# Bidirectional RWKV-7 triangular inverse: the transposed state kept by a vector transpose in place of its own matmuls

## What is computed

```python
def step(S, inp):                       # one token; two directions z, 16 heads of 64 channels
    r_t, w_t, k_t, v_t, a_t, b_t = inp
    sa = jnp.einsum('zbhvk,zbhk->zbhv', S, a_t)
    S = S * w_t[..., None, :] + sa[..., :, None] * b_t[..., None, :] + v_t[..., :, None] * k_t[..., None, :]
    return S, jnp.einsum('zbhvk,zbhk->zbhv', S, r_t)

xs = (shared(r), time_major(decay), time_major(k_dir), shared(v), shared(-kk), time_major(b_dir))
_, ys = lax.scan(step, jnp.zeros((2, B, H, N, N), f32), xs)
```

## Time and profile before

| | us |
|---|---|
| median of 3 runs | 1345.2 |
| lowest and highest | 1340.76, 1352.06 |
| the profiled execution | 1351.68 |
| its span, from first to last instruction | 1349.8 |
| scan stage in it, tile 0 to the end of tile 7 | about 854 to 1105 |

### The profile page before, as it was taken

How to read it: one execution, slowest core, us unless ns; L and a number is a source line. 1 busy time by engine, 2 the same in 40 slices (tenths; PEclk the granted TensorE clock), 3 DMA queues, 4 the chain that set the end, 5 groups by cost and what they waited for, 6 DMA issues and landing times.

```text
span 1349.8 us, 33102 instructions
## 1 busy us (share of the span) xinstructions
PE 1259.2 (93%) x14080; PEld 1131.4 (84%) x14080; DVE 919.8 (68%) x1270; ACT 644.7 (48%) x1045; POOL 442.0 (33%) x220
## 2 busy tenths in 40 slices
PE   8999999999899999899997899888888889899998
PEld 5899999878799999799996898877777777799998
DVE  7666667786877776766667985656555546866654
ACT  5544446452644455644445368233333333555553
POOL 1344442211244443344443000543334303344442
PEclk9999999999999999999998899789999989999999
DMA  8355555323355555455555342010000012555553
GB/s 332 141 185 184 186 185 173 123 86 140 141 186 186 186 186 200 174 186 186 186 186 187 101 181 95 3 50 4 4 4 4 3 50 95 195 188 186 186 184 119
DMA packets 18676, 188.34 MB, mean 140 GB/s; under 512 B 2064, under 2 KB 2576, under 8 KB 3600
## 3 DMA queue, kind: packets, MB, share of 16 engines
q1 hardware_dynamic: 18576, 186.84, 38.5%
HBM read 185.78 MB, written 1.05 MB: 138 GB/s over the span
## 4 chain that ended last, share of the span: by engine, by line
PE 75%; DVE 15%; ACT 5%; issue 3%; POOL 1%; DMA 0%; SPq 0%; DVEq 0%; ACTq 0%
PE gu_bank L257 22%; PE gu_bank L259 11%; PE bank L236 7%; PE bank L238 7%; PE bank L237 7%; PE bank L1380 5%; PE gu_bank L1411 4%; PE gu_bank L236 3%; PE gu_bank L237 2%; PE gu_bank L238 2%; DVE WL L193 2%; ACT WH L186 1%; DVE XSQ L407 1%; POOL raw L1893 1%; PE gu_bank L1380 1%
## 5 line engine op out<-in xcount | busy, mean ns | idle before, releaser
L202 POOL TENSOR_TENSOR WL<-raw,WH 128x1024 fp32r<-128x1024 f32 x102 | 342.0, 3354 | 597.1 <-ACT WH L187 575.3
L257 PE MATMUL gu_bank<-HX,WH 128*128 128x512 f32 x1408 | 508.2, 403 | 13.8 <-DVE WL L193 12.1
L259 PE MATMUL gu_bank<-HX,WL 128*128 128x256 f32 x1408 | 398.5, 283 | 0.0
L193 DVE TENSOR_TENSOR WL<-raw,WH 128x2048 fp32r<-128x2048 f32 (+1 forms) x114 | 252.6, 2215 | 137.8 <-ACT WH L186 137.7
L257 PEld LDWEIGHTS gu_bank<-HX,WH 128*128 128x128 f32 x1408 | 267.9, 190 | 78.5 <-DVE WL L193 8.5
L259 PEld LDWEIGHTS gu_bank<-HX,WL 128*128 128x128 f32 x1408 | 269.6, 191 | 0.2
L186 ACT ACTIVATE WH<-raw 128x2048 fp32r<-128x2048 f32 (+1 forms) x114 | 204.6, 1795 | 23.4 <-PE gu_bank L238 13.5
L236 PE MATMUL bank<-PH,WH 128*128 128x256 f32 (+1 forms) x720 | 202.0, 284 | 1.0 <-ACT arena L1942 1.0
L237 PE MATMUL bank<-PL,WH 128*128 128x256 f32 (+1 forms) x720 | 201.9, 283 | 0.0
L238 PE MATMUL bank<-PH,WL 128*128 128x256 f32 (+1 forms) x720 | 201.8, 283 | 0.0
L438 ACT ACTIVATE work<-work 128x256 f32<-128x256 f32 x88 | 36.8, 418 | 278.0 <-DVE work L490 278.0
(11 more groups left out here) (311 smaller groups left out, 2028.2 us busy)
## 6 DMA issues: line engine op xcount, KB each, us to landing
raw<-stream_in SPq DMA_DIRECT2D x114, 1536.0 KB, 6.5
cst<-const_in SPq DMA_DIRECT2D x1, 1568.0 KB, 16.9
X<-xT_in SPq DMA_DIRECT2D x1, 1024.0 KB, 5.6
raw<-stream_in SPq DMA_DIRECT2D x1, 1024.0 KB, 7.6
arena<-hconst_in SPq DMA_DIRECT2D x2, 512.0 KB, 10.8
out<-X SPq DMA_DIRECT2D x4, 256.0 KB, 2.4
arena<-hconst_in SPq DMA_DIRECT2D x1, 768.0 KB, 13.9
arena<-fw_in SPq DMA_DIRECT2D x1, 512.0 KB, 8.4
```

Source lines behind the costliest of these rows:

```text
L193: nc.vector.tensor_tensor(WL[:, slot, :cut], raw[:, slot, :cut], WH[:, slot, :cut].bitcast(fp32), ALU.subtract).then_inc(lo_ready, 1)
L202: (eng or nc.gpsimd).tensor_tensor(WL[:, slot, cut:end], raw[:, slot, cut:end], WH[:, slot, cut:end].bitcast(fp32), ALU.subtract).then_inc ...
L257: nc.tensor.matmul(out[:, :], WH[:, slot, w:w + P], HX[:, x, :, :].rearrange("p i t -> p (i t)"), start=k == 0, stop=False)
L259: return nc.tensor.matmul(out[:, L:2 * L], WL[:, slot, w:w + P], HH[:, x, :], start=False, stop=k == CT - 1)
```

## The change

T0 is no longer updated by matmuls. Up to level 3 the non-zero part of T is made of blocks of at most 32x32, so T0 is T1 with each 32x32 block transposed, and VectorE has an instruction that does that for 128x256 elements (`turned`). It runs once per z in the tile's head and once per z behind each of the levels 0 to 3, each time behind the addition that finishes T1. The addition is now on T1's one side alone, half as many elements. The crossed product in the head (CBANK), its mask and its waits are gone. All products are plain now: `zee` and the T1 update too. `update` waits on a new semaphore, `t0_ready`. Apart from that, `pe_s` carries the old state through the identity in one 128-column product per head instead of two of 64 columns.

```diff
-        def crossed(dst, cols, w, x):
...
-        def side_heads(dst, at, n, w, x, cross):
+        def side_heads(dst, at, n, w, x):
 
             for h in range(2):
-                r, o = halves(h, cross)
-                out_ = dst[o, at:at + CH // 2].rearrange("p (k b) -> p k b", b=LEVELS[n])
+                r = slice(HD * h, HD * h + HD)
+                out_ = dst[r, at:at + CH // 2].rearrange("p (k b) -> p k b", b=LEVELS[n])
                 last = nc.tensor.matmul(out_, w[r], x[r], start=True, stop=True)
...
             pe.wait_ge(uu_ready, 4 * t + i + 1)
+            if i:
+                heads(bank[4], slice(4 * CH, 6 * CH), istack, SCH[i % 2].rearrange("p z v -> p (z v)"), stop=False)
             for z, u in enumerate(units(i)):
                 dst, cols = bank[4], at64(4 + z)
-                if i:
-                    heads(dst, cols, istack, SCH[i % 2][:, z], stop=False)
...
             for z in range(2):
-                if z == 1 and t > 1:
-                    pe.wait_ge(gn_c, t - 1)
-                elif z == 1 and t == 0:
-                    pe.wait_ge(vd_read, 2)
                 for c in range(NCH):
                     u = z * NCH + c
-                    heads(ZBANK[z], at64(c), AR[p][:, u, 0], beta[:, u])
-                    last = crossed(CBANK[z], at64(c), AR[p][:, u, 0], beta[:, u])
+                    last = heads(ZBANK[z], at64(c), AR[p][:, u, 0], beta[:, u])
                 last.then_inc(a_done, 1)
...
                 if n == 0:
                     pe.wait_ge(aq_read, 2 * t + z + 1)
+                pe.wait_ge(t0_ready, 10 * t + 2 * n + z + 1)
                 for c in range(NCH):
-                    if n < len(LEVELS) - 1:
-                        side_heads(ZBANK[z], P + c * CH // 2, n, ZB[n][:, z, c], side(TQ[:, z, 0, c], n, 1 - late(z)), False)
-                        zb = side(ZB[n][:, z, c], n, late(z))
-                    else:
-                        zb = ZB[n][:, z, c].rearrange("p (k b) -> p k b", k=1)
-                    last = side_heads(DBANK[z], P + c * CH // 2, n, TQ[:, z, 0, c], zb, True)
+                    zb = ZB[n][:, z, c]
+                    zb = side(zb, n, late(z)) if n < len(LEVELS) - 1 else zb.rearrange("p (k b) -> p k b", k=1)
+                    last = side_heads(DBANK[z], P + c * CH // 2, n, TQ[:, z, 0, c], zb)
...
+            def turned(z, ready):
+
+                dve.wait_ge(t_ready, ready)
+                nc.vector.transpose(TQ[:, z, 0].rearrange("p c s -> p (c s)"), TQ[:, z, 1].rearrange("p c s -> p (c s)"))\
+                    .then_inc(t0_ready, 1)
...
+            own.settle()
             for z in range(2):
-                dve.wait_ge(a_done, 2 * t + z + 1)
-                own(tt(TQ[:, z, 0], CBANK[z][:, 0:L].rearrange("p (c s) -> p c s", c=NCH), mask64("first", z * CH),
-                       ALU.mult))
-                own.settle()
-                tq = TQ[:, z].rearrange("p i c s -> p (i c) s")
-                tt(tq, tq, eye, ALU.add).then_inc(t_ready, 1)
+                tt(TQ[:, z, 1], TQ[:, z, 1], eye, ALU.add).then_inc(t_ready, 1)
+            for z in range(2):
+                turned(z, 12 * t + z + 1)
...
-                        tq = both_sides(TQ[:, z], b, late(z))
-                        tt(tq, tq, gu_bank[:, z, :, P:L].rearrange("p i (k b) -> p i k b", b=b), ALU.add).then_inc(t_ready, 1)
+                        t1 = side(TQ[:, z, 1].rearrange("p c s -> p (c s)"), n, late(z))
+                        tt(t1, t1, DBANK[z][:, P:L].rearrange("p (k b) -> p k b", b=b), ALU.add).then_inc(t_ready, 1)
+                        turned(z, 12 * t + 2 * n + z + 3)
```

More of the change, by code:

```diff
@@ L1245, in build @@
         aq_done, aq_read, bq_done, abd_ready = sem("aq_done"), sem("aq_read"), sem("bq_done"), sem("abd_ready")
-        xl_ready, z_done, zb_ready, d_done, t_ready = (sem(n) for n in "xl_ready z_done zb_ready d_done t_ready".split())
+        xl_ready, z_done, zb_ready, d_done, t_ready, t0_ready = (
+            sem(n) for n in "xl_ready z_done zb_ready d_done t_ready t0_ready".split())
         zb_clear, qf_ready = sem("zb_clear"), sem("qf_ready")
@@ L1392, in late @@
             return 1 - z
-        def halves(h, cross):
-            a, b = slice(HD * h, HD * h + HD), slice(HD * (1 - h), HD * (1 - h) + HD)
-            return (a, b) if cross else (a, a)
-        def crossed(dst, cols, w, x):
+        def side_heads(dst, at, n, w, x):
             for h in range(2):
-                r, o = halves(h, True)
-                last = nc.tensor.matmul(dst[o, cols], w[r], x[r], start=True, stop=True)
-            return last
-        def side_heads(dst, at, n, w, x, cross):
-            for h in range(2):
-                r, o = halves(h, cross)
-                out_ = dst[o, at:at + CH // 2].rearrange("p (k b) -> p k b", b=LEVELS[n])
+                r = slice(HD * h, HD * h + HD)
+                out_ = dst[r, at:at + CH // 2].rearrange("p (k b) -> p k b", b=LEVELS[n])
                 last = nc.tensor.matmul(out_, w[r], x[r], start=True, stop=True)
@@ L1474, in pe_s @@
             pe.wait_ge(uu_ready, 4 * t + i + 1)
+            if i:
+                heads(bank[4], slice(4 * CH, 6 * CH), istack, SCH[i % 2].rearrange("p z v -> p (z v)"), stop=False)
             for z, u in enumerate(units(i)):
                 dst, cols = bank[4], at64(4 + z)
-                if i:
-                    heads(dst, cols, istack, SCH[i % 2][:, z], stop=False)
                 heads(dst, cols, KTK[p][:, u], VTK[p][:, u % NCH], start=i == 0, stop=False)
-                last = heads(dst, cols, BTK[p][:, u], UCH[:, z], start=False)
+                last = heads(dst, cols, BTK[p][:, u], UCH[:, z], start=False, stop=i == 0 or z == 1)
             last.then_inc(s_done, 1)
@@ L1538, in zee @@
             def zee(n, z, c):
-                return side_heads(ZBANK[z], c * CH // 2, n, XL[n][:, z, c], side(TQ[:, z, 1, c], n, late(z)), True)
+                return side_heads(ZBANK[z], c * CH // 2, n, XL[n][:, z, c], side(TQ[:, z, 1, c], n, late(z)))
             def zee_wait(n, z):
@@ L1771, in dve_yt @@
             nc.vector.tensor_scalar(tile_of(R, t), bank[6][:, 0:L], 1.0, None, ALU.mult).then_inc(yt_ready, 1)
[L1773 to L1777 removed]
         def dve_tile(dve, t, p, chunks, ahead, own):
             tt, q = nc.vector.tensor_tensor, 1 - p
[L1781 removed]
+            eye = istack.rearrange("p (o s) -> p o s", o=1).broadcast_to([P, NCH, CH])
             def units_of(b):
                 return b[:, :].rearrange("p (c s) -> p c s", c=NCH)
+            def turned(z, ready):
+                dve.wait_ge(t_ready, ready)
+                nc.vector.transpose(TQ[:, z, 0].rearrange("p c s -> p (c s)"), TQ[:, z, 1].rearrange("p c s -> p (c s)"))\
+                    .then_inc(t0_ready, 1)
             for z in range(2):
```

6 lines of the change are left out of this document (removed).

## The result

The changed kernel takes 1339.85 us (median of 20 runs, 1334.88 to 1342.97), the kernel before, in 20 runs beside it, 1351.39 us. The ratio is 0.9918, with a 95% interval of 0.9903 to 0.9932: faster by 0.8%, 11.5 us, where the sum had said 3.9 us slower. It is inside the range, but on the other side of the forecast; by the prediction's own bound of 1% it counts as no difference. The prediction had put its +3.9 on the 1345.2 us of three runs; on the 1351.39 of twenty it would have read 1355.3, 15.4 us above what came. The profiled execution took 1336.9 us, with a span of 1335.0 us against 1349.8.

The account below looks back on a forecast made before the run. A chain changing sides between TensorE and VectorE sets the pace, neither being full. Seven tiles x (1.35 + 0.64) = +13.9 us, tile 0 +1.5, waits without a name -11.5: +3.9, 1349 us; range 1335 to 1365 for 8 in 10.

Parts of the forecast that it names:

- the prediction's own bound of 1%: Whole kernel: 13.5 us, about what a measurement of this kernel can tell from no change.
- lost pairs: TensorE, levels 0 to 3: plain zee no longer runs beside pe_r and pe_tr, +1.35 us a tile.
- tile 0: First tile, without chunk steps: two transposes on the path and a level 2 group at half clock, +1.5 us.
- waits without a name: TensorE's "issue" waits in dense levels, read as running out of loaded instructions: 11.5 of 14.3 us go.
- Removed array time 0: TensorE: the removed T0 and crossed head products ran beside others, so array time saved is about 0.
- VectorE, +0.64 us a tile: Addition plus transpose on the path behind levels 0 and 3, z = 1: +0.32 us each.
- The two in the head: Tile's head: two transposes replace a mask and half of a wider addition, and the copy waits for TensorE: nothing.
- the two places with +0.32 us each: VectorE, z = 1: behind level 0, ahead of prefix and copy; behind level 3, ahead of gate matmuls and next tile.
- slower by the clock: Rival: fewer matmuls bring more half-clock stretches, 1357 us with one more per tile, 1366 with two; chance 0.24.
- more than one tile in three: Sign in the changed trace: the forecast is wrong if more tiles than this have a stretch at half clock.
- the 1.2 that was taken: TensorE: cost in us of one half-clock stretch, from tile 4's 31.52 us where its neighbours were 30.3.
- 0.60 for no change: Chance of the same time: 0.53 for the sum as it stands (1341 to 1357) plus 0.07 from the clock.

Follow-up runs that it names:

- Dead products: Changed kernel with 64 unread products a tile added to the updates of levels 0 to 3: 1348.8 us with 32 columns each, 1351.5 us with one column.
- The kernel with all products plain: Kernel before without the 64 T0 products a tile, zee and the update's products plain instead of crossed, VectorE and GpSimd as before: 1345.2 us.
- the run with dead wide additions: Changed kernel with two unused 128x512 additions on VectorE ahead of the head's transposes, in the seven tiles with chunk steps: 1343.45 us.
- all three moves: Changed kernel with three VectorE steps issued earlier or later: level 0's z = 1 transpose, alpha's first half, AQ's masks: 1330.8 us.
- Two such moves: Changed kernel with alpha's first half ahead of level 3's second addition and AQ's masks ahead of level 0's copy: 1328.3 us.

## Why the prediction was wrong

The sum was 9.5 (lost pairs) + 4.5 (VectorE) + 1.5 (tile 0) - 11.5 (waits without a name) = +3.9. The runs give, each against before: without T0 products -19.9; then update plain +6.2; zee plain +7.5; then the rest of the change, VectorE's part and the head's 16 crossed products, -5.3 (from -6.2 to -11.5). By the intervals of the ratios a difference between two of these runs is uncertain by 3.5 us (the last) to 7 us (the update's), so the undisturbed tiles stand beside them.

- **Waits without a name**: right in kind and nearly in size. 14.3 us went to 0.7 in the run and to 0 in the changed kernel, where 11.5 of 14.3 were taken. Dead products bring them back, by their number, and each of these waits ends 1.2 to 1.6 us behind the landing of an instruction packet. The prediction had only read this from packets and rates; these runs show it.
- **Removed array time 0**: right. The 6.3 us beyond "issue" in the run without T0 products are partners for the crossed update, and the changed kernel, whose update is plain, does not get them: -6.3 and +6.2 in medians, 3.3 us by undisturbed tiles.
- **Lost pairs, +9.5**: right in mechanism and somewhat high. The groups took 0.95 and 1.40 us as forecast, an undisturbed tile loses 1.43 us with zee's pairs in the changed kernel and 1.21 in the kernel without T0 products and with the update plain; over all, zee's part is 7.5 us.
- **VectorE, +0.64 us a tile**: this is the step that failed, by 9.8 of the 15.4 us between 3.9 and -11.5: +4.5 us were forecast, -5.3 came. The durations were right (0.45 us, +0.35 a pair). What was wrong is "The two in the head replace a mask and half of a wider addition, and the copy of level 0 waits for TensorE behind them; nothing". The kernel with all products plain and the changed kernel have the same products in the levels, so their undisturbed tiles, 30.07 and 29.72 us, show what the rest of the change did: -0.35 us a tile. TensorE, zee of level 0 (z = 1 alone, then both together), all plain and changed:
```profile
949.08 0.65 PE L1411 MATMUL gu_bank<-scan,raw 64*64 64x32 f32 x16 [0.34 <-POOL raw L1892]
1006.62 1.07 PE L1400 MATMUL gu_bank<-scan,raw 64*64 64x32 f32 x32
```
and VectorE's chunk copy of level 0, which waits for TensorE in both:
```profile
950.04 0.29 DVE L1760 COPY work<-bank 128x128 f32<-128x128 f32 x1 [1.60 <-PE bank L1380]
1008.00 0.29 DVE L1741 COPY work<-bank 128x128 f32<-128x128 f32 x1 [1.94 <-PE bank L1381]
```
The wide additions of the old head ran beside GpSimd's first two masks, which took 1.28 and 1.17 us; zee for z = 1 waited for the second one. In the changed kernel these masks take 0.89 and 0.72 us and zee runs on. The copy comes 3.43 us behind the tile's first mask with the old head and 2.92 with the new one: the head, put at nothing, gains 0.51 us a tile. The same contention has two more parts. The scan behind the second addition of level 0 takes 0.65 us instead of 0.82, and alpha's first pair 1.14 instead of 1.46, since both meet less of GpSimd's work. So of the two places with +0.32 us each one cost about 0.2 and the other nothing, and +0.64 became -0.35: 7 us in seven tiles. The other 2.8 of the 9.8 us are within the uncertainty of the medians, and no row places them. The signs stood in the trace: the wait for GpSimd is in the earlier trace rows in every tile, and the two scans of one line, of the same shape, had two durations before (VectorE's groups by form, 885 to 1100 us):
```profile
L1709 DVE TENSOR_TENSOR_SCAN arena<-cst,arena 128x256 f32<-128x256 f32 x6 | 5.5, 922 | 0.0
L1709 DVE TENSOR_TENSOR_SCAN scan<-cst,arena 128x256 f32<-128x256 f32 x6 | 4.0, 660 | 0.0
```
I took both as fixed. No run puts the old head alone back on the path: the run with dead wide additions shows that they slow the masks, but its time is the late copy.
- **Tile 0, +1.5**: wrong; from GpSimd's first mask in it to that in tile 1 it was 28.0 us before and 27.8 after.
- **The clock**: the granted clock of the page is as before (0.973 before, 0.976 after), and the rival "slower by the clock" did not come. Its sign was met all the same: a stretch of 3.4 us at half clock lies in tiles 1, 2 and 3 of the first trace, three of seven where "more than one tile in three" was to prove the forecast wrong. It lies in one of seven in the second trace of the changed kernel, and in three of seven before (tiles 1, 4 and 7). So the sign did not tell the cases apart. What one costs is 0.6 us in tile 3 above (30.34 against 29.72 us) and up to 1.6 in other runs (29.90 against 28.33 with all three moves); the 1.2 that was taken lies between.
- **The chances**: a near balance of two large terms was given 0.60 for no change, and the sign was wrong. The price of VectorE's part was bounded at 0.15 to 0.65 us a step, above nothing; that the head's edits could gain was left out, and with it the sign. That the time fell inside the range of 1335 to 1365 is luck: the range started from 1345.2, which is 6 us below the kernel's median in twenty runs, and from 1351.4 it would have read 1341 to 1371, with 1339.85 outside.

## What to carry to other kernels

- A sum of costs and gains per engine is not complete until it is asked which operations of other engines run beside the ones removed. Look in the trace for an operation of one form with two durations, and see what ran beside the long ones.
- Matmul instructions that cost no array time can still cost time, where small products are issued faster than they are loaded. "issue" waits scattered over dense groups, with the instruction queue busy, are the sign; the number of instructions is what to cut.
- Price a removed pair against the neighbours as they will be, not as they are; and when an engine idles for a later one, let it do there what otherwise lies behind it. Two such moves gave as much as the change itself (11.5 us).
- Dead work put into idle time must be shown to fit there before its price is read: slowed to 1.16 us an addition, it made the next copy late, and the time it cost was its own.

## What was unexpected of the hardware

- VectorE and GpSimd slowed each other here, in operations with both inputs in SBUF: GpSimd's mask 128x256 took 0.72 us alone and up to 1.28 us beside VectorE's 128x512 addition, and that addition took 0.73 us on average before and 1.16 as dead work; VectorE's scalar_tensor_tensor 128x256 took 0.40 us alone, 0.61 and 0.84 on average beside GpSimd's 128x512; the scan 0.65 and, on average, 0.92. The transposes of 128x256 in the levels, 0.45 us long and with one input, left the masks beside them at 0.72, and so did VectorE's 128x512 masks of BQ, one of whose inputs lies in PSUM (1008.66 and 1008.87 us in the changed kernel). The Trainium skill, "GPSIMD Engine Reference", section "8. Key points", says that GpSimd shares its interfaces to SBUF with VectorE and that VectorE's instructions with two SBUF inputs contend with it. These rows agree in both directions, and this is the rule that the prediction should have weighed.
- Dead products of one column paced the update as those of 32 columns did: 0.68 and 0.67 us for 32 rows.
- 128 MATMUL rows more a tile, of one column, cost 11.7 us in all, with 8.5 us of "issue". The Trainium skill, "Runtime: NRT & Kernel Launch", section "Instruction fetch mechanics", says that an engine's instructions are refilled in blocks of 16 KB while it runs, and that this is mostly hidden. The queue's packets are of that size here (34 of them, 0.56 MB), but with dense small products it is not hidden: 14.3 us in seven tiles before, none after, and every one of these waits ends 1.2 to 1.6 us behind a landing.
